# Expert layers: the scatter put one round later, the token sums seeded inside round 0, and the embedding joined on VectorE

## What is computed

```python
# reference, cut
for g in range(N_GROUPS_2):                                    # 4 groups of 8 experts
    hg = silu(einsum('nd,edf->nef', xt, w_g[g])) * einsum('nd,edf->nef', xt, w_u[g])
    y = y + einsum('nef,efd->nd', hg * comb[:, g, :, None], w_d[g])
...
ffn = hierarchical_moe(x, ...)
ple = sigmoid(x @ w_ple_gate[i]) * (p[i] @ w_ple[i])
x = layer_norm(ALPHA * x + ffn + ple, ln2_g[i], ln2_b[i])      # second block
```

## Time and profile before

| | |
|---|---|
| median of 3 runs | 2486.99 us |
| span of the profiled execution (the page gives no other time for it) | 2489.0 us |
| TensorE matmul busy | 2270.0 us, 91% |
| TensorE weight load busy | 1350.7 us, 54% |
| VectorE busy | 859.7 us, 35% |
| ScalarE busy | 415.1 us, 17% |
| mean granted TensorE clock | 0.963 |
| moved by DMA | 602.21 MB, mean 242 GB/s |

### The profile page before, as it was taken

How to read it: one execution, slowest core, us unless ns; L and a number is a source line. 1 busy time by engine, 2 the same in 40 slices (tenths; PEclk the granted TensorE clock), 3 DMA queues, 4 the chain that set the end, 5 groups by cost and what they waited for, 6 DMA issues and landing times. The chain is left out here.

```text
span 2489.0 us, 40588 instructions
## 1 busy us (share of the span) xinstructions
PE 2270.0 (91%) x17537; PEld 1350.7 (54%) x17537; DVE 859.7 (35%) x1712; ACT 415.1 (17%) x747; POOL 22.5 (1%) x114
## 2 busy tenths in 40 slices
PE   5979999799988999998998899999998899899996
PEld 3759888464437678666443455444443455444442
DVE  6885676641114121324111262132111352131112
ACT  1023432010001000321000123121000224021001
POOL 0000000000000000000000000000000000000000
PEclk8989999889999999999999999989999999999999
DMA  9900000789996665226999533466999443567995
GB/s 378 336 1 3 4 3 4 280 326 421 420 420 250 235 220 192 78 75 243 421 421 419 189 127 119 186 241 238 421 420 397 140 134 118 186 239 300 421 421 233
DMA packets 139922, 602.21 MB, mean 242 GB/s; under 512 B 34840, under 2 KB 37976, under 8 KB 84960
## 3 DMA queue, kind: packets, MB, share of 16 engines
q1 hardware_dynamic: 126912, 591.66, 60.7%
q10 hardware_dynamic: 12576, 7.89, 1.2%
q0 software_dynamic: 256, 0.02, 0.0%
HBM read 598.46 MB, written 1.05 MB: 241 GB/s over the span
## 5 line engine op out<-in xcount | busy, mean ns | idle before, releaser
L2360 PE MATMUL ps<-store 128*32 128x512 f32 (+1 forms) x2816 | 319.0, 606 | 26.8 <-DMA store<-in_moe_w_up 15.1
L3055 PE MATMUL ps<-store,x_features 128*128 128x512 f32 x704 | 322.7, 602 | 4.8 <-PEq L2878 2.6
L403 PE MATMUL ps<-store 128*128 128x512 f32 x480 | 215.3, 610 | 11.0 <-PEq L752 7.9
L2360 PEld LDWEIGHTS ps<-store 128*32 128x32 f32 x2816 | 89.0, 112 | 248.9 <-issue 248.9
L3055 PEld LDWEIGHTS ps<-store,x_features 128*128 128x128 f32 x704 | 128.2, 192 | 136.4 <-issue 134.2
L2378 PE MATMUL ps<-store 128*32 128x512 f32 (+1 forms) x1408 | 160.2, 595 | 36.2 <-DVE store L2483 36.2
L2318 PEld LDWEIGHTS ps<-store 128*128 128x128 f32 x1408 | 162.1, 193 | 42.9 <-issue 33.5
L2478 DVE TENSOR_TENSOR store<-ps,store 128x256 f32<-128x256 f32 x44 | 18.7, 425 | 480.6 <-ACT store L2426 480.6
L2318 PE MATMUL ps<-store 128*128 128x128 f32 x1408 | 170.5, 279 | 6.1 <-DVE store L2457 6.1
L433 PE MATMUL ps<-x_features,store 128*128 128x256 f32 x768 | 166.8, 379 | 0.9 <-PEq L752 0.9
L403 PEld LDWEIGHTS ps<-store 128*128 128x128 f32 x480 | 93.3, 196 | 128.8 <-issue 128.8
(11 more groups left out here) (434 smaller groups left out, 2300.7 us busy)
## 6 DMA issues: line engine op xcount, KB each, us to landing
store<-in_moe_w_gate SPq DMA_DIRECT2D x64, 1024.0 KB, 18.6
store<-in_moe_w_up SPq DMA_DIRECT2D x64, 1024.0 KB, 20.7
store<-in_moe_w_down SPq DMA_DIRECT2D x64, 1024.0 KB, 23.1
store<-in_w_exp_gate SPq DMA_DIRECT2D x64, 1024.0 KB, 17.0
store<-in_w_exp_up SPq DMA_DIRECT2D x64, 1024.0 KB, 18.5
store<-in_w_exp_down SPq DMA_DIRECT2D x64, 1024.0 KB, 19.8
store<-in_ada_w SPq DMA_DIRECT2D x48, 1024.0 KB, 13.5
store<-in_w_in SPq DMA_DIRECT2D x40, 1024.0 KB, 5.0
```

Of the source, the lines that this page charges most:

```text
L403: mm = pe.matmul(k.ps[:, set_ * 4 + tile * 2 + h, 0:n], xT[:, s, tile * P:(tile + 1) * P], w[:, kk, c0:c0 + n], start=(s == 0), stop=(s == ...
L2360: mm = pe.matmul(v3(k.ps[w * CAP:(w + 1) * CAP, 6, :], 2, F), xe[:, q % 2, s, w], both[:, :, s * F:(s + 1) * F], start=(s == 0), stop=(s = ...
L3055: mm = pe.matmul(k.ps[:, 2 * (j % 2) + tile, :], x, row[:, 0:HALF], start=(s_ == 0), stop=(s_ == K8 - 1))
```

## The change

- `start_sums` and `weigh` leave the routing phases; the embedding's products with its gates leave `gate_route_phase`, and ScalarE waits there for its own sigmoids.
- The experts' buffers are laid out by one function, `expert_buffers`, that both phases call. The gates lie where the second half of the gathered tokens and the results will be.
- `gatedT` has three buffers in place of two (`q % 3`).
- In layers 2 and 3 VectorE multiplies embedding and gates behind `build(1)` and adds ALPHA times the tokens, into `k.x`, and then signals `sums_seeded`.
- TensorE seeds only tile 1, with two matmuls behind round 0's first layer; the first scatter starts the sums of tile 0. L2405 goes.
- `scatter(q - 1)` runs between `turn(q)` and `second_layer(q)`, and the last scatter at the end. The waits for the copies of the results move with it, and `take_tokens` from round 2 on has waits of its own for them.
- Tile 0's tokens are added on VectorE behind the layer: an addition in place of a copy in `moe_sums_phase`, and in `layer_norm_phase` a reduction that adds two operands, with the subtraction then reading SBUF.

```diff
@@ route_parts, route_phase, gate_route_phase
-    def start_sums(pe):
-        pe.wait_ge(k.route_steps.sem, k.route_steps.at(4))
-        for b in range(4):
-            pe.matmul(k.ps[:, b, :], k.ident[:, :] if first else weigh, k.x[:, b // 2, (b % 2) * HALF:(b % 2 + 1) * HALF],
-                      start=True, stop=True)
...
-            link(pool.memset(weigh, 0.0))
-            link(pool.affine_select(out=weigh, in_=weigh, ...
...
-            r.start_sums(pe)
...
+            act.wait_ge(k.gates_ready.sem, k.gates_ready.at(TILES))
...
-            for tile in range(TILES):
-                vec.wait_ge(k.gates_ready.sem, k.gates_ready.at(tile + 1))
-                k.vec_chain.link(vec, vec.tensor_tensor(ple[:, tile], ple[:, tile], gates[:, tile], MUL))
+def expert_buffers(k):
+    c = Carver(k.region, k.region_w, k.moe_end)
...
+    b.gatedT = v3(c.take(3 * T), 3, T)
...
+    b.xe = c.take(2 * K8 * P).rearrange("p (b s w n) -> p b s w n", b=2, s=K8, w=WIDE)
+    b.out = c.take(D)
...
+    b.gates = v3(k.region[:, c.at - TILES * D:c.at], TILES, D)
@@ experts_phase, TensorE
             def take_tokens(q):
                 wait_pair(pe, k.slots_built, q)
+                if q > 1:
+                    wait_pair(pe, k.out_moved0, q - 2)
+                    wait_pair(pe, k.out_moved1, q - 2)
...
                 wait_pair(pe, k.hidden_moved, q)
-                if q:
+                if q == ROUNDS - 1:
                     wait_pair(pe, k.out_moved0, q - 1)
                     wait_pair(pe, k.out_moved1, q - 1)
...
-                                  out[:, h * HALF:(h + 1) * HALF], start=False, stop=True, skip_group_check=True)
+                                  out[:, h * HALF:(h + 1) * HALF], start=(q == 0 and tile == 0), stop=True,
+                                  skip_group_check=True)
+            def start_sums():
+                if extra is not None:
+                    pe.wait_ge(k.sums_seeded.sem, k.sums_seeded.at(1))
+                for h in range(2):
+                    pe.matmul(k.ps[:, 2 + h, :], k.ident[:, :], k.x[:, 1, h * HALF:(h + 1) * HALF], start=True, stop=True)
...
                 first_layer(q)
+                if q == 0:
+                    start_sums()
                 if q + 1 < ROUNDS:
                     take_tokens(q + 1)
                 turn(q, True, q + 1 < ROUNDS)
+                if q:
+                    scatter(q - 1)
                 second_layer(q)
-                scatter(q)
-                if q == 1 and extra is not None:
-                    for b in range(4):
-                        pe.matmul(k.ps[:, b, :], k.ident[:, :], extra[:, b // 2, ...
+            scatter(ROUNDS - 1)
@@ experts_phase, VectorE
             build(1)
+            if extra is not None:
+                for tile in reversed(range(TILES)):
+                    k.vec_chain.link(vec, vec.tensor_tensor(extra[:, tile], extra[:, tile], b.gates[:, tile], MUL))
+                    k.vec_chain.link(vec, vec.scalar_tensor_tensor(out=k.x[:, tile], in0=k.x[:, tile], scalar=ALPHA,
+                                                                   in1=extra[:, tile], op0=MUL, op1=ADD))
+                vec.sem_inc(k.sums_seeded.sem, 1)
@@ moe_sums_phase
-            k.vec_chain.link(vec, vec.tensor_copy(k.x[:, 0], bank(k, 0, 2)))
+            k.vec_chain.link(vec, vec.tensor_tensor(k.x[:, 0], bank(k, 0, 2), k.x[:, 0], ADD))
@@ layer_norm_phase
-            if product is not None:
-                link(vec.tensor_tensor_reduce(k.x[:, 0], k.x[:, 0], bank(k, 0, 2), 1.0, 0.0, ADD, ADD, mean[:, 0:1]))
-            else:
-                link(vec.tensor_reduce(mean[:, 0:1], sums(0), X, ADD))
+            link(vec.tensor_tensor_reduce(k.x[:, 0], k.x[:, 0], bank(k, 0, 2), 1.0, 0.0, ADD, ADD, mean[:, 0:1]))
...
-            link(vec.tensor_scalar(k.x[:, 0], sums(0), mean[:, 0:1], None, SUB))
+            link(vec.tensor_scalar(k.x[:, 0], k.x[:, 0], mean[:, 0:1], None, SUB))
```

More of the change, by code:

```diff
@@ L272, in make_core @@
     (k.route_logits, k.route_turned, k.route_ranks, k.route_steps, k.route_exp, k.route_rows, k.route_constants,
-     k.embed_turned, k.embed_ready, k.gates_ready) = (
+     k.embed_turned, k.embed_ready, k.gates_ready, k.sums_seeded) = (
         Signal(sem(name)) for name in (
             "route_logits", "route_turned", "route_ranks", "route_steps", "route_exponents", "route_rows", "route_constants",
-            "embed_turned", "embed_ready", "gates_ready"))
+            "embed_turned", "embed_ready", "gates_ready", "sums_seeded"))
     k.over_landed = [sem(f"overflow_landed{i}") for i in range(2 * DEPTH)]
@@ L1921, in route_parts @@
     k.moe_end = c.at
-    before, ones, weigh = (c.take(P) for _ in range(3))
+    before, ones = (c.take(P) for _ in range(2))
     chosen, rank, gates, over = (v3(c.take(TILES * EX), TILES, EX) for _ in range(4))
@@ L2000, in constants @@
         link(pool.memset(ones, 1.0))
-        if not first:
-            link(pool.memset(weigh, 0.0))
-            link(pool.affine_select(out=weigh, in_=weigh, pattern=[[-1, P]], compare_op=ALU.not_equal, fill=ALPHA, base=0,
-                                    channel_multiplier=1))
         link(pool.memset(before, 1.0))
@@ L2142, in route_phase @@
     r.close()
+def expert_buffers(k):
+    c = Carver(k.region, k.region_w, k.moe_end)
+    b = Core()
+    b.slots, b.gated = (c.take(TILES * P).rearrange("p (t w n) -> p t w n", t=TILES, w=WIDE) for _ in range(2))
+    b.gatedT = v3(c.take(3 * T), 3, T)
+    b.silu_out, b.hid = c.take(F), c.take(F)
+    b.hidT = v3(c.take(2 * P), 2, P)
+    b.xe = c.take(2 * K8 * P).rearrange("p (b s w n) -> p b s w n", b=2, s=K8, w=WIDE)
+    b.out = c.take(D)
+    assert c.at <= KEPT
+    b.gates = v3(k.region[:, c.at - TILES * D:c.at], TILES, D)
+    assert TILES * D == K8 * P + D
+    return b
 def gate_route_phase(k, i, name, ple, move, row, off):
@@ L2149, in gate_route_phase @@
     r = route_parts(k, i, 0, 2)
-    gates = v3(k.region[:, KEPT - TILES * D:KEPT], TILES, D)
+    gates = expert_buffers(k).gates
     with k.nc.Block() as block:
@@ L2218, in experts_phase @@
     n0 = k.starts[f"moe{i}"]
-    c = Carver(k.region, k.region_w, k.moe_end)
-    slots, gated = (c.take(TILES * P).rearrange("p (t w n) -> p t w n", t=TILES, w=WIDE) for _ in range(2))
-    gatedT = v3(c.take(2 * T), 2, T)
-    silu_out, hid = c.take(F), c.take(F)
-    hidT = v3(c.take(2 * P), 2, P)
-    out = c.take(D)
-    xe = c.take(2 * K8 * P).rearrange("p (b s w n) -> p b s w n", b=2, s=K8, w=WIDE)
-    assert c.at <= KEPT
-    c.at = KEPT
+    b = expert_buffers(k)
+    slots, gated, gatedT, silu_out, hid, hidT, xe, out = b.slots, b.gated, b.gatedT, b.silu_out, b.hid, b.hidT, b.xe, b.out
+    c = Carver(k.region, k.region_w, KEPT)
     over_w = v3(c.take(3 * SLOT), 3, SLOT)
@@ L2389, in scatter @@
                     for tile in range(TILES):
-                        pe.matmul(k.ps[:, 2 * tile + h, :], gatedT[:, q % 2, tile * P:(tile + 1) * P],
-                                  out[:, h * HALF:(h + 1) * HALF], start=False, stop=True, skip_group_check=True)
+                        pe.matmul(k.ps[:, 2 * tile + h, :], gatedT[:, q % 3, tile * P:(tile + 1) * P],
+                                  out[:, h * HALF:(h + 1) * HALF], start=(q == 0 and tile == 0), stop=True,
[5 more added lines that the diff above has]
+                    pe.matmul(k.ps[:, 2 + h, :], k.ident[:, :], k.x[:, 1, h * HALF:(h + 1) * HALF], start=True, stop=True)
             take_tokens(0)
@@ L2400, in _ @@
                 turn(q, True, q + 1 < ROUNDS)
+                if q:
+                    scatter(q - 1)
                 second_layer(q)
-                scatter(q)
-                if q == 1 and extra is not None:
-                    for b in range(4):
-                        pe.matmul(k.ps[:, b, :], k.ident[:, :], extra[:, b // 2, (b % 2) * HALF:(b % 2 + 1) * HALF],
-                                  start=False, stop=True, skip_group_check=True)
+            scatter(ROUNDS - 1)
             overflow(pe, general)
@@ L2463, in move_gated @@
                 wait_pair(vec, k.turned, q)
-                vec.tensor_copy(gatedT[:, q % 2], k.ps[:, 7, T:2 * T]).then_inc(k.gated_moved.sem, 1)
+                vec.tensor_copy(gatedT[:, q % 3], k.ps[:, 7, T:2 * T]).then_inc(k.gated_moved.sem, 1)
             def take_tokens(q):
@@ L2509, in experts_phase @@
     k.turned.close(ROUNDS + 1)
+    if extra is not None:
+        k.sums_seeded.close(1)
 def moe_sums_phase(k):
```

3 lines of the change are left out of this document (1 added, 2 removed).

## The result

The kernel after takes 2499.86 us (median of 13 runs, 2492.99 to 2505.11), the kernel before in the same series 2487.94 us (13 runs, 2481.75 to 2494.84). The ratio is 1.0041, 95% interval 1.0029 to 1.0054: slower by 10.2 us, 7.2 to 13.4. The change reaches its aim and loses time all the same. If the same holds for before (an estimate), its profiled execution took 2490.7 us, 2.8 over the median of its runs, while that of after is 1.7 under its own median: so the pair lies closer together than the medians do.

A forecast was written before the change was run, and what follows sets the result against it. Weight transfers were taken to bound the kernel by setting round 9. Layer terms of 2.2, 2.2 and at most 0.1 each in layers 2 and 3 gave 4.4, plus 1.5 for the clock: +5.9 us, 2494.9, range 2489.0 to 2498.5.

The forecast's parts named there:

- second rival: Clock loss at each round 9 and a long restart in layer 0: +11.2 us, 2498.2; chance 0.06.
- start of layer 0: TensorE idles longer once seeding leaves routing, so layer 0 starts at a lower clock: +1.6 us, bounds 0 and 2.4.
- start of layer 1: Longer TensorE idle after routing adds nothing more, as layer 1 already pays for a low clock: 0.
- end of routing, layers 2 and 3: Routing ends with ScalarE's second sigmoid, so VectorE's masks start sooner: -2.14 us each, bounds 0 and -2.7.
- tail, clock aside, four layers: Round 9 to layer end: round 8's scatter adds 3.63 us, waits of 0.85 and 0.60 go: +2.18 a layer.
- layer 0's end covered by SyncE: SyncE's last issues already delay the phase behind layer 0, so its longer tail shows as only +0.6 us.
- clock at round 9: A wait of 3.8 us (2.3 after a slow round 8) costs one layer in four: +1.5 us, bounds 0 and 6.0.
- first layer of round 0 to round 9: Rounds 0 to 8 shorten to 18.5 us, but transfers hide it all: 0.
- Transfers set round 9: First refill to round 9 stays 176.8 us whatever TensorE does between, since weight transfers set when round 9 starts.
- first rival: The shorter rounds come through because TensorE's removed waits count: 38.9 us faster, 2448.1; chance 0.08.
- fourth rival: The second layer still idles 0.85 and 0.60 us behind the scatter, tails +3.63: 2498.7; chance 0.02.
- the third: No visible difference: no clock loss at round 9, layer 0 starts near full clock: +2.8 us, 2489.8; chance 0.22 with neighbours.

The follow-up runs named there:

- caught_up: The changed kernel, but round 8 runs both round 7's scatter and its own, and rounds 9 and 10 have the old order: 2490.81 us, ratio 1.0005.
- awake_nine: The changed kernel with 8 filler matmuls ahead of the wait for round 9's weights: 2491.88 us, ratio 1.0003 to the kernel before.
- tokens_sooner: Changed kernel with the scatter back in its own round, 24 filler matmuls behind the ranks (layers 0, 1), round 10's gathering ahead of round 9's wait: ratio 0.9977.
- awake: The changed kernel with 24 more filler matmuls behind the rank matmuls of layers 0 and 1: 2494.45 us, ratio 1.002 to the kernel before.

## Why the prediction was right, and where its terms were off

The forecast was +5.9 us, slower, within +2 to +11.5. The interval of the ratio, +7.2 to +13.4, has its middle at +10.2 and its upper end past the range; the raw median after, 2499.86, lies 1.4 over the stated upper end, with before 0.95 above the median that the forecast started from. Part of the agreement is luck: of the terms below, starts and clock were put 5.3 us too low and the tails 2.7 too high, and +10.2 lies nearer to the second rival's +11.2 than to the forecast. The steps, against the profiled pair:

| step | forecast, us | measured, us |
|---|---|---|
| start of layer 0 | +1.6 (0 to 2.4) | +2.95 |
| start of layer 1 | 0 | +1.01 |
| end of routing, layers 2 and 3 | -2.14 each | -2.19 each |
| tail, clock aside, four layers | +2.18 each | +1.51, 1.51, 1.51, 1.44 |
| layer 0's end covered by SyncE | -1.6 | -1.60 |
| clock at round 9 | +1.5 | +4.42 |
| first layer of round 0 to round 9 | 0 | +0.35 in all |
| all else | 0 | -1.36 |
| sum | +5.9 | +7.36 |

**Transfers set round 9: right, and shown.** Distances unchanged with 33 us of waits removed; with less to load they fall to 167.0 to 170.7 us, and the change takes 12 to 16 us more off them. With full weights they moved by more than 0.5 us only where TensorE came late, by 1 us behind a slow round 8 (caught_up, awake_nine) and by 2 in tokens_sooner. The first rival was refuted by its own test: it gives 42 us where the share falls under 1. The Trainium skill (Perfetto Trace Analysis, section Optimization Strategies) would have the engines sped up that block the critical path when the matmul engine idles for them. The prediction's first rival took every such wait to be on that path. Here they were not: 33 of 36.2 us of such idle time gone, ratio 1.0041.

**The tail: mechanism right, size off.** Forecast was 3.63 - 0.85 - 0.60. Round 9 shortens by 1.23 (740.50 - 721.15 = 19.35 in the earlier trace rows and before's timeline, 1367.20 - 1349.08 = 18.12 after), not 0.85, and round 10 grows by 2.74 to the last matmul, not 3.03. The gap ahead of the removed wait went with it, 0.16 us (from L2340's start to L2378's there were 1.22 us with 0.84 of wait, from L2339's to L2389's 0.22), and so did 0.22 in the two groups behind: 3.53 us from scatter to second layer and 3.46 from there to the next first layer, where before had 3.57 for the second layer and 3.64 for the scatter behind it. The term was 0.67 too dear in each layer.

**The starts: mis-sized.** The bound of 2.4 for layer 0 came from the lower clock over part of the work; the idle stretch of 6.65 us cost 2.95. Taking layer 1 at nothing more, since it pays already, was wrong: 2.26 us of idle had cost it 1.63, 6.63 cost it 2.64. A longer idle stretch costs more even where the clock falls either way. The run awake shows this cause by removing it.

**The clock at round 9: the largest error.** One loss of 1.5 was counted; two fell, of 2.72 and 1.70. The trace of before spoke against a single one already. The prediction has it agree with the rival "for the wait of 2.84 us alone"; but all five waits over 2.5 us of the first layers of before were followed by a slow one, and the five under 2.5 us by a fast one. Besides the 2.84 these were a 3.28 in round 8 of layer 3 (8.77 us) and, in round 7 of layer 0 and round 8 of layers 1 and 2:

```profile
675.15 8.48 PE L2360 MATMUL ps<-store 128*32 x64 [2.56 <-DMA store<-in_moe_w_up]
...
1323.58 8.53 PE L2360 MATMUL ps<-store 128*32 x64 [4.26 <-DMA store<-in_moe_w_up]
...
1868.01 8.77 PE L2360 MATMUL ps<-store 128*32 x64 [3.23 <-DMA store<-in_w_exp_up]
```

The wait there was put at 3.8 us, which by the count of 146 waits is nearly always slowed. The waits were 5.62, 2.39, 3.59 and 1.10. The longest stands where round 8 ran at full clock, behind 2.36 us of idle; the other three stand behind a slow round 8 (waits of 3.90, 4.04 and 5.26), and two of them were short enough. So the second rival was half right in its number of losses (two of four, at 2.2 each and not 1.5) and right in the long restart of layer 0. The Trainium skill (TensorE: Matmul & The Clock Gate, section Loop structure matters more than you think) has matmuls go cold behind a long DMA wait in a loop, 8 us in its picture. The trace agrees on the mechanism, and here waits from 2.5 us on did it.

**The rest.** The end of routing up to the masks, SyncE's cover, VectorE's four operations inside round 0 and the sums behind the layers came as worked out. The -1.36 in all else is mainly -3.66 between layers 0 and 1 (396.0 against 392.3) and +2.28 between layers 2 and 3, the slower router matmuls shown above. The cause of the first was not traced. Such parts vary by up to 5 us among the kernels run (390.8 to 396.0 between layers 0 and 1), and the profiled execution of before had the longest.

The fourth rival is out (3.0 us left of the wait), and the third too (the ratio's interval begins at 1.0029).

## What to carry to other kernels

Measure the distance between a stretch's first refill and its last round that waits for a transfer: if it is the same whatever the matmul engine does in between, waits inside it are free as long as that engine still arrives before the transfer does, and moving work later means moving it out from under that cover, where it costs in full. The same picture gives the gain: what stands behind the last such wait and could stand ahead of it (here the gathering of tokens) is worth moving forward. And when an instruction leaves an engine that is idle next, add the idle time up: the matmul engine pays for it with its clock.

## What the runs showed of the hardware beyond that

- The price of idle time is graded and nearly certain beyond some length: 3 of 65 waits under 2.5 us slowed the next first layer, 77 of 81 above (table of 146), and a loss was 1.3 to 3.0 us.
- Two VectorE operations on 128x1024 that read SBUF alone take 1.22 us each, and the addition that reads PSUM 1.23: the joining on VectorE costs the same as the copy it replaced.
- Filler matmuls of 5.61 us behind the ranks bring the tokens' gathering from 6.76 to 3.84 us. They delay nothing that follows: they end 1.22 us before the gathering starts, which waits for VectorE's masks.
- 23.9 MB less to load in a layer (7/8 of 26 down blocks of 1.049 MB; in all 506.79 MB in place of 602.21) made before 38 us faster by the ratio, without a change to any other engine's work.
